# A two-layer float32 transformer kernel: weights of three products woven in pairs and loaded with a step of two, the value product streamed 512 columns wide

## The chip, the cores and the metric

The kernel runs on one core of a Trainium2 chip. The metric is the device time of one execution in microseconds, the median of several runs; lower is better.

## The reference, cut to what matters

Two transformer layers on 256 tokens of width 2048 in float32, at batch 1. The first has stick-breaking and forgetting attention and then PEER: every token picks 16 of 16384 experts in each of 8 heads. The kernel computes the expert part densely: all 16384 expert inputs, weighted by a gate that is zero where an expert isn't picked.

```python
def block(hb):                                   # PEER, first layer
    q = (hb @ w_query).reshape(PEER_BLOCK, PEER_HEADS, 2, D_KEY // 2)
    s = jnp.einsum('thpc,hpnc->thpn', q, sub_keys).astype(jnp.float32)
    top_s, top_i = lax.top_k(s, PEER_TOPK)
    ...
    best_s, best_j = lax.top_k(cand_s, PEER_TOPK)
    idx = jnp.take_along_axis(cand_i, best_j, axis=-1)
    g = jax.nn.softmax(best_s, axis=-1)
    a = jax.nn.gelu(jnp.einsum('thkd,td->thk', jnp.take(u, idx, axis=0), hb), approximate=False)
    return jnp.einsum('thk,thkd->td', (g * a).astype(hb.dtype), jnp.take(v, idx, axis=0))
```

The second layer has block attention, a state-space branch and a feed-forward part of hidden width 5632, with an up projection to 2 x 5632 (`w_up`), a three-tap convolution along the tokens, a gate and a down projection (`w_down`).

## The kernel before, in words

All activations stand transposed, with features on the 128 partitions and the 256 tokens along the free dimension. All large weights come as one stream of 1152 halves (`STREAM`): a half is 128 partitions x 1024 float32, 512 KB. SyncE fetches each half into a ring of four (`raw`). ScalarE copies it, quarter by quarter (512 columns), into a rounded float32r tile `whi` (L1061, L1150), VectorE subtracts to get the low part `wlo` (L1557, L1701; L1901 beside the selection), and TensorE forms each product as three float32r matmuls: high x high, high x low, low x high (`three`, L502, L507, L508; in the value product L651, L659, L661). `whi` and `wlo` hold two halves; semaphore `quarters_used` gives a quarter back to ScalarE, `lo_ready` hands one to TensorE and returns a slot of `raw` to SyncE.

In a dense product (`dense_turn`: expert product `peer_u`, and `w_up`) the weights are the stationary operand, 128 columns of a quarter at a time, and the activations stream, 256 columns. One output chunk of 128 features takes 16 x 3 matmuls. `peer_u` has 128 chunks, `w_up` 88. The first 16 chunks of `w_up` (`early_chunk`) stream 258 columns from the tile `early` while the normalisation is still going on. In the value product (`spread_tokens`, `peer_v`) it is the other way round: the gated expert values of 128 tokens are stationary (`ev_hi`, `ev_lo`) and the weight rows stream, as two sides of 256 columns to a bank; all eight banks of PSUM accumulate over 128 rows of experts. The down product (`spread`, `w_down`) keeps its weights stationary.

Some turns have a cut: one of their matmuls is issued as 240 and 16 columns (`CUT = 240`, the arguments `cuts` and `cut`, the list RESET in the product `w_in_2`).

The activation parts (`parts`, `split_view`) all lie in one area; the third argument is their offset in bytes. The area, `raw`, `whi`, `wlo` and `big` begin at the same residue modulo 256. A row of 256 float32 is 1024 bytes, a row of the first product's tile (`hhi`, 272 columns) 1088. So for the expert product the weights stand 64 bytes after the stream modulo 256 (0 - 192), for the value product also 64 (64 - 0), and for `early`, which begins 80 bytes after a multiple of 256, they stand at 176.

Beside the first half of the expert product, VectorE also selects the experts: `route_turn`, 16 turns, each with 16 low parts (`low`) written out between the steps of the selection. GpSimd then scatters the gates to memory and later multiplies them into the activated values, one expert row per 5.4 us. From turn 14 of the value product on, VectorE adds up the products for the second layer's modulation from 1 MB tiles of `w_mod` (L2030), which GpSimd fetches. After the value product the eight banks go to SBUF, TensorE turns them (L901), and VectorE adds them to `x2` (L2042); this is a stretch in which TensorE waits.

Of the kernel before, what the change touches and what calls it, by code (L numbers as in the profile page):

```python
# [11 lines left out]
ALU = mybir.AluOpType  # L12
# [3 lines left out]
P = 128  # L16
SEQ = 256
# [3 lines left out]
KC = D // P  # L21
HEADS = 8
RING = 4
HALF = 1024
# [5 lines left out]
N_SUB = 128  # L30
# [63 lines left out]
def quarter(q):  # L94

    return slice(q * HALF // 2, (q + 1) * HALF // 2)


def build(nc, d, out):
    ctx = ExitStack()  # L100
    with ctx:
# [9 lines left out]
        at = -(-nc.sbuf_base // 32) * 32  # L111
# [9 lines left out]
        def parts(name, rows, beyond, row=SEQ):  # L121
            return [split_view(name + part, at + k * KC * KEYS * 4 + beyond, rows, row, SEQ)
                    for k, part in enumerate(("_hi", "_lo"))]

        sb_hi, sb_lo = parts("sb_parts", 8, 192)
        tok_hi, tok_lo = parts("tok_parts", KC, 192)
        in_hi_, in_lo_ = parts("in_parts", KC, 192)
        ya_hi, ya_lo = parts("ya_parts", 8, 192)
        at_hi, at_lo = parts("at_parts", 8, 8 * SEQ * 4 + 192)
        mg_hi, mg_lo = parts("mg_parts", 8, 8 * SEQ * 4 + 192)  # L130
        up_hi, up_lo = parts("up_parts", KC, 192)
        dn_hi, dn_lo = parts("dn_parts", 2, 192)
        ev_hi, ev_lo = parts("ev_parts", 2, 64)
        raw = sb("raw", [P, RING, HALF])
        whi = sb("whi", [P, PAIRS, HALF], F32R)
        wlo = sb("wlo", [P, PAIRS, HALF], F32R)
# [33 lines left out]
        PS = ctx.enter_context(nc.psum_tensor("PS", [P, 8, 512], F32))  # L170
# [22 lines left out]
        x2 = region(128 * SEQ - KC * SEQ, KC, SEQ)  # L193
# [303 lines left out]
        def _(pe):  # L497
            CUT = 240
# [47 lines left out]
            def dense_turn(name, chunk0, width, g, after=None, inputs=None, halves=None, shift=0, tiles=None, cuts=()):  # L546

                h0_ = FIRST[name]
                if True:
                    for c in range(4):  # L550
                        pe.wait_ge(banks_free, g * 4 + (chunk0 + c + 1))
                        for half in range(2):
                            for kc in range(8):
                                if kc % 4 == 0:

                                    pe.wait_ge(lo_ready, g * 16 + 2 * (RING + h0_ + 2 * c + half) + kc // 4 + 1)
                                    if inputs is not None and c == 0:
                                        pe.wait_ge(in_ready, inputs + 2 * half + kc // 4 + 1)
                                if tiles is not None and c == 0 and (half + kc == 0 or half * 8 + kc >= 12):
                                    pe.wait_ge(tiles, max(half * 8 + kc + 1, 12))  # L560
                                at_ = slice(kc * P, (kc + 1) * P)
                                hi, lo = tuple(t[:, half * 8:, :] for t in ((tok_hi, tok_lo) if name == "peer_u" else (up_hi, up_lo))) if halves is None else halves[half]
                                last = three(PS[:, (c + shift) % 4, 0:width], whi[:, half, at_], wlo[:, half, at_], hi[:, kc, :], lo[:, kc, :],
                                             half == 0 and kc == 0, half == 1 and kc == 7, c in cuts and half == 0 and kc == 3)
                                if kc % 4 == 3:
                                    last.then_inc(quarters_used, 1)
                        if after is not None:
                            after(c)
# [60 lines left out]
                with pe.Fori(4, turns) as g:  # L629
                    body(g, False, False)  # L630

            def spread_tokens(name, turns, staged, cuts):

                h0_ = FIRST[name]

                def body(g, opening, cut=False):
                    for b in range(4):
                        opens = opening and b == 0
                        e_hi, e_lo = ev_first if opens else (ev_hi[:, b % 2, :], ev_lo[:, b % 2, :])
                        pe.wait_ge(stage_lo, g * 4 + (staged + b + 1))  # L640
                        for half in range(2):
                            if opens:
                                pe.wait_ge(banks_free, 4 + 88 + N_SUB - 2 + 2 * half)
                            for q in range(2):
                                pe.wait_ge(lo_ready, g * 16 + 2 * (RING + h0_ + 2 * b + half) + q + 1)
                                for t in range(2):
                                    o_ = slice(t * P, (t + 1) * P)
                                    for side in range(2):
                                        bank = PS[:, t * 4 + half * 2 + q, side * SEQ:(side + 1) * SEQ]
                                        at_ = slice((2 * q + side) * SEQ, (2 * q + side + 1) * SEQ)  # L650
                                        pe.matmul(bank, e_hi[:, o_], whi[:, half, at_], start=opens and side == 0,  # L651
                                                  stop=False, skip_group_check=True)
                                        if cut and b == 1 and half == 0 and q == 1 and t == 0 and side == 0:
                                            for part in (slice(0, CUT), slice(CUT, SEQ)):
                                                pe.matmul(bank[:, part], e_hi[:, o_],
                                                          wlo[:, half, (2 * q + side) * SEQ + part.start:(2 * q + side) * SEQ + part.stop],
                                                          start=False, stop=False, skip_group_check=True)
                                        else:
                                            pe.matmul(bank, e_hi[:, o_], wlo[:, half, at_], start=False, stop=False,  # L659
                                                      skip_group_check=True)  # L660
                                        last = pe.matmul(bank, e_lo[:, o_], whi[:, half, at_], start=False,  # L661
                                                         stop=False, skip_group_check=True)
                                last.then_inc(quarters_used, 1)

                body(0, True)
                for at, until in zip((0,) + cuts, cuts + (turns,)):
                    if at:
                        body(at, False, True)
                    with pe.Fori(at + 1, until) as g:
                        body(g, False)  # L670

            def mod_sum_rows(acc, count, bank):

# [18 lines left out]
            for g in range(4):  # L692
                pe.wait_ge(squares, g + 1)
                for q in range(4):
                    last = pe.matmul(PS[32 * q:32 * q + 32, 7, 0:KEYS], ones[:, 0:32], sq0[:, 4 * g + q, :], start=g == 0, stop=g == 3)
# [150 lines left out]
            for n in range(KC):  # L846
                pe.wait_ge(banks_free, 56 + n + 1)
                for half in range(2):
                    hi, lo = (fox_hi, fox_lo) if half == 0 else (sb_hi, sb_lo)
                    for kc in range(8):  # L850
# [4 lines left out]
                        at_ = slice(kc * P, (kc + 1) * P)  # L855
# [20 lines left out]
            for n in range(8):  # L876
                t, q4 = n // 4, n % 4
# [14 lines left out]
            mod_turn(2, 7)  # L892
            dense("peer_u", 88, SEQ, (17, 18), cuts=(1,))
            dense("peer_u", 88, SEQ, (18, N_SUB // 4))
            spread_tokens("peer_v", N_SUB // 4, 0, (2, 10, 15, 17, 22, 26))
            for q in range(4):
                pe.wait_ge(acc_copied_a, q + 1)
                pe.wait_ge(acc_copied_v, q + 1)
# [5 lines left out]
            for c in range(KC):  # L904
                q = c % 4
                pe.wait_ge(squares_pv, c // 4 + 1)
                last = pe.matmul(PS[32 * q:32 * q + 32, 0, 0:SEQ], ones[:, 0:32], sqb[:, c, :], start=c < 4, stop=c >= KC - 4)
# [115 lines left out]
            def early_chunk(g, c):  # L1023

                pe.wait_ge(banks_free, 336 + 4 * g + c + (3 if g == 0 and c < 2 else 1))
                for kc in range(KC):
                    half = kc // 8
                    if kc % 4 == 0:
                        pe.wait_ge(lo_ready, 2 * (RING + FIRST["w_up"] + 8 * g + 2 * c + half) + kc // 4 % 2 + 1)
                    if g == 0 and c == 0 and (kc == 0 or kc >= 12):  # L1030
                        pe.wait_ge(early_lo, max(kc + 2, 13))
                    at_ = slice(kc % 8 * P, (kc % 8 + 1) * P)
                    last = three(PS[:, c, 0:SEQ + 2], whi[:, half, at_], wlo[:, half, at_], early[:, 0, kc, 0:SEQ + 2],
                                 early[:, 1, kc, 0:SEQ + 2], kc == 0, kc == KC - 1)
                    if kc % 4 == 3:
                        last.then_inc(quarters_used, 1)
# [502 lines left out]
        def _(dv):  # L1539
# [444 lines left out]
            t = lam_t  # L1984
# [53 lines left out]
            for q in range(4):  # L2038
                dv.wait_ge(acc_turned, q + 1)
                for a in range(2):  # L2040
                    part = x2[:, 4 * q + 2 * a:4 * q + 2 * a + 2, :]
                    i = dv.tensor_tensor(part, part, PS[:, 4 * a + q, :].rearrange("p (b t) -> p b t", b=2), ALU.add)  # L2042
                i.then_inc(x2_ready, 1)
            dv.wait_ge(sums_by_four, 2)
            dv.tensor_scalar(rstd[:, 1, 0:SEQ], PS[:, 0, 0:SEQ], 1.0 / 32, None, ALU.mult).then_inc(sums_kept, 1)
# [420 lines left out]
```

## Time and profile before

| | |
|---|---|
| Median of 3 runs | 3401.7 us (3396.45 to 3410.36) |
| Span of the profiled execution, first to last instruction | 3397.2 us, 4.5 us below that median |
| TensorE busy | 3362.4 us (99%), 29184 matmuls |
| VectorE, ScalarE, GpSimd busy | 2500.3, 1963.3, 736.1 us |
| Mean granted TensorE clock | 0.997 |

"Busy" of TensorE is the time in which at least one matmul was in flight. Matmuls overlap, so their rate is read from how many start in a stretch, or from the times at which they start. A weight load has a row of its own kind (PEld). A releaser is the instruction whose semaphore ended a wait.

### The profile page before, as it was taken

What the parts mean: (1) busy time and instruction counts of PE and PEld (TensorE: products, weight loads), DVE (VectorE), ACT (ScalarE), POOL (GpSimd) and SP (SyncE); (2) the same over time, 40 slices, a digit from 0 to 9 for tenths busy, and PEclk for the clock granted to TensorE, in tenths of its full rate; (3) what the DMA queues carried; (4) which work ended last, traced back from release to release, by engine and by line L of the source; (5) the groups of instructions that cost most, each with busy time, mean ns of one, the idle gap of its engine ahead of it and who ended that gap; (6) DMA issues with size and microseconds to landing.
All of it is one profiled execution on the core that took longest, in us unless ns stands there. A gap on an engine that the chain in (4) does not pass through costs nothing.

```text
span 3397.2 us, 80038 instructions
## 1 busy us (share of the span) xinstructions
PE 3362.4 (99%) x29184; PEld 3319.9 (98%) x29184; DVE 2500.3 (74%) x4438; ACT 1963.3 (58%) x3483; POOL 736.1 (22%) x709
## 2 busy tenths in 40 slices
PE   8999999999999999999999999999999999999999
PEld 7999999999999999999999998999999999999999
DVE  7886688788875555676788879998667776666555
ACT  5456655677765555555555556765565665555554
POOL 1001130377777723555000000000000000000000
PEclk9999999999999999999999999999999999999999
DMA  8867788577777766877898864545555555555555
GB/s 325 335 221 253 248 299 303 161 187 190 186 193 194 194 204 225 271 244 249 320 341 338 335 218 132 176 160 183 162 189 192 187 190 192 192 191 196 187 192 179
DMA packets 234085, 758.61 MB, mean 223 GB/s; under 512 B 60072, under 2 KB 63664, under 8 KB 221104
## 3 DMA queue, kind: packets, MB, share of 16 engines
q1 hardware_dynamic: 167328, 608.57, 52.8%
q0 software_dynamic: 62624, 139.63, 15.0%
q10 hardware_dynamic: 3952, 7.91, 0.7%
q8 instruction: 125, 2.05, 0.2%
q14 instruction: 56, 0.46, 0.0%
HBM read 732.78 MB, written 21.11 MB: 222 GB/s over the span
## 4 chain that ended last, share of the span: by engine, by line
PE 94%; DVE 4%; ACT 1%; issue 1%; DMA 1%; DVEq 0%; SPq 0%; ACTq 0%
PE PS L502 24%; PE PS L508 23%; PE PS L507 23%; PE PS L651 7%; PE PS L661 7%; PE PS L659 7%; DVE wlo L1701 1%; DVE big L1695 0%; PE PS L934 0%; DMA raw<-peer_v_dram 0%; PE PS L761 0%; DVE big L1628 0%; PE PS L923 0%; PE PS L880 0%; PE PS L946 0%
## 5 line engine op out<-in xcount | busy, mean ns | idle before, releaser
L1061 ACT ACTIVATE whi<-raw 128x512 fp32r<-128x512 f32 x1864 | 1157.8, 630 | 1022.8 <-PE PS L508 652.3
L1557 DVE TENSOR_TENSOR wlo<-raw,whi 128x512 fp32r<-128x512 f32 x1480 | 1024.9, 706 | 605.9 <-ACT whi L1061 585.6
L502 PE MATMUL PS<-tok_parts_hi,whi 128*128 128x256 f32 x2048 | 569.4, 278 | 0.8 <-ACT big L1286 0.7
L508 PE MATMUL PS<-tok_parts_hi,wlo 128*128 128x256 f32 x2048 | 568.3, 277 | 0.0
L651 PE MATMUL PS<-whi,ev_parts_hi 128*128 128x256 f32 x2032 | 561.8, 276 | 1.1 <-DVE wlo L1557 1.1
L661 PE MATMUL PS<-whi,ev_parts_lo 128*128 128x256 f32 x2032 | 562.1, 277 | 0.0
L507 PE MATMUL PS<-tok_parts_lo,whi 128*128 128x256 f32 x2030 | 561.7, 277 | 0.0
L659 PE MATMUL PS<-wlo,ev_parts_hi 128*128 128x256 f32 x2026 | 559.9, 276 | 0.0
L1701 DVE TENSOR_TENSOR wlo<-raw,whi 128x512 fp32r<-128x512 f32 x564 | 381.6, 695 | 129.2 <-ACT whi L1150 84.1
L434 POOL DMA_INDIRECT gates_dram<-big x256 | 427.0, 1668 | 200.2 <-issue 91.1
L1150 ACT ACTIVATE whi<-raw 128x512 fp32r<-128x512 f32 x436 | 271.4, 629 | 250.4 <-PE PS L508 247.5
L502 PEld LDWEIGHTS PS<-tok_parts_hi,whi 128*128 128x128 f32 x2048 | 384.6, 188 | 3.8 <-DVE wlo L1901 1.7
L508 PEld LDWEIGHTS PS<-tok_parts_hi,wlo 128*128 128x128 f32 x2048 | 385.4, 188 | 0.0
L651 PEld LDWEIGHTS PS<-whi,ev_parts_hi 128*128 128x128 f32 x2032 | 381.5, 188 | 1.5 <-DVE wlo L1557 1.5
L661 PEld LDWEIGHTS PS<-whi,ev_parts_lo 128*128 128x128 f32 x2032 | 381.5, 188 | 0.0
L507 PEld LDWEIGHTS PS<-tok_parts_lo,whi 128*128 128x128 f32 x2030 | 381.2, 188 | 0.0
L659 PEld LDWEIGHTS PS<-wlo,ev_parts_hi 128*128 128x128 f32 x2026 | 380.9, 188 | 0.0
L508 PE MATMUL PS<-up_parts_hi,wlo 128*128 128x256 f32 x1152 | 318.0, 276 | 0.0
L502 PE MATMUL PS<-up_parts_hi,whi 128*128 128x256 f32 x1152 | 318.0, 276 | 0.0
L507 PE MATMUL PS<-up_parts_lo,whi 128*128 128x256 f32 x1151 | 317.7, 276 | 0.0
L502 PE MATMUL PS<-in_parts_hi,whi 128*128 128x256 f32 x1024 | 289.6, 283 | 5.1 <-DVE wlo L1701 3.2
L508 PE MATMUL PS<-in_parts_hi,wlo 128*128 128x256 f32 x1024 | 286.3, 280 | 0.0
(552 smaller groups left out, 8201.3 us busy)
## 6 DMA issues: line engine op xcount, KB each, us to landing
raw<-peer_u_dram SPq DMA_DIRECT2D x256, 512.0 KB
raw<-peer_v_dram SPq DMA_DIRECT2D x256, 512.0 KB
raw<-w_in_dram SPq DMA_DIRECT2D x240, 512.0 KB
big<-w_mod_dram POOLq DMA_DIRECT2D x96, 1024.0 KB, 6.6
raw<-w_up_dram SPq DMA_DIRECT2D x176, 512.0 KB
raw<-w_down_dram SPq DMA_DIRECT2D x88, 512.0 KB
raw<-w_out_dram SPq DMA_DIRECT2D x64, 512.0 KB
gates_dram<-late POOLq DMA_DIRECT2D x16, 1024.0 KB, 9.0
```

Of the source, the lines that this page charges most:

```text
L434: pool.indirect_dma_start(gates_flat, bass.IndirectOffsetOnAxis(ap=pick_at[:, u, n:n + 1], axis=0), pick_weight[:, u, n:n + 1], None, comp ...
L502: pe.matmul(out, hi, rhi, start=start, stop=False, **more)
L507: pe.matmul(out, hi, rlo, start=False, stop=False, **more)
L508: return pe.matmul(out, lo, rhi, start=False, stop=stop, **more)
L651: pe.matmul(bank, e_hi[:, o_], whi[:, half, at_], start=opens and side == 0, stop=False, skip_group_check=True)
L659: pe.matmul(bank, e_hi[:, o_], wlo[:, half, at_], start=False, stop=False, skip_group_check=True)
L661: last = pe.matmul(bank, e_lo[:, o_], whi[:, half, at_], start=False, stop=False, skip_group_check=True)
L1061: f(whi[:, m % PAIRS, quarter(q)], raw[:, m % RING, quarter(q)], ACT.Copy).then_inc(hi_ready, 1)
L1150: f(whi[:, m % PAIRS, quarter(q)], raw[:, m % RING, quarter(q)], ACT.Copy).then_inc(hi_ready, 1)
L1557: dv.tensor_tensor(wlo[:, m % PAIRS, quarter(q)], raw[:, m % RING, quarter(q)], whi[:, m % PAIRS, quarter(q)], ALU.subtract).then_inc(lo_r ...
L1701: dv.tensor_tensor(wlo[:, m % PAIRS, quarter(q)], raw[:, m % RING, quarter(q)], whi[:, m % PAIRS, quarter(q)], ALU.subtract).then_inc(lo_r ...
```

## The change

1. The weights of `peer_u` and `w_up` are laid out in memory in pairs: within each 256 columns of a half, the columns of two stationary tiles alternate (`woven`). The matmuls read one of the two with a step of two (`dense_turn` without `halves`, and `early_chunk`).
2. The tiles that stream against them begin at offset 96 in place of 192. The weights then stand 160 bytes from the stream modulo 256. `early` isn't moved and stays at 176.
3. In the value product the stationary tile takes every second token, at offset 160 in place of 64. The stream is one matmul of 512 columns in place of two of 256, and the six turns with a cut are gone.
4. As the output rows of the value product are now alternate tokens, the add into `x2` reads and writes `x2` with a step of two.

```diff
-        tok_hi, tok_lo = parts("tok_parts", KC, 192)
+        tok_hi, tok_lo = parts("tok_parts", KC, 96)
-        up_hi, up_lo = parts("up_parts", KC, 192)
+        up_hi, up_lo = parts("up_parts", KC, 96)
-        ev_hi, ev_lo = parts("ev_parts", 2, 64)
+        ev_hi, ev_lo = parts("ev_parts", 2, 160)
...
-                                at_ = slice(kc * P, (kc + 1) * P)
+                                at_ = slice(kc // 2 * 2 * P + kc % 2, (kc // 2 + 1) * 2 * P, 2) if halves is None else slice(kc * P, (kc + 1) * P)
...
                                 for t in range(2):
-                                    o_ = slice(t * P, (t + 1) * P)
-                                    for side in range(2):
-                                        bank = PS[:, t * 4 + half * 2 + q, side * SEQ:(side + 1) * SEQ]
-                                        at_ = slice((2 * q + side) * SEQ, (2 * q + side + 1) * SEQ)
-                                        pe.matmul(bank, e_hi[:, o_], whi[:, half, at_], start=opens and side == 0,
-                                                  stop=False, skip_group_check=True)
...
-                                        last = pe.matmul(bank, e_lo[:, o_], whi[:, half, at_], start=False,
-                                                         stop=False, skip_group_check=True)
+                                    o_ = slice(t, SEQ, 2)
+                                    bank = PS[:, t * 4 + half * 2 + q, :]
+                                    pe.matmul(bank, e_hi[:, o_], whi[:, half, quarter(q)], start=opens, stop=False,
+                                              skip_group_check=True)
+                                    pe.matmul(bank, e_hi[:, o_], wlo[:, half, quarter(q)], start=False, stop=False,
+                                              skip_group_check=True)
+                                    last = pe.matmul(bank, e_lo[:, o_], whi[:, half, quarter(q)], start=False, stop=False,
+                                                     skip_group_check=True)
...
-            spread_tokens("peer_v", N_SUB // 4, 0, (2, 10, 15, 17, 22, 26))
+            spread_tokens("peer_v", N_SUB // 4, 0)
...
-                    at_ = slice(kc % 8 * P, (kc % 8 + 1) * P)
+                    at_ = slice(kc % 8 // 2 * 2 * P + kc % 2, (kc % 8 // 2 + 1) * 2 * P, 2)
...
-                    part = x2[:, 4 * q + 2 * a:4 * q + 2 * a + 2, :]
-                    i = dv.tensor_tensor(part, part, PS[:, 4 * a + q, :].rearrange("p (b t) -> p b t", b=2), ALU.add)
+                    part = x2[:, 4 * q + 2 * a:4 * q + 2 * a + 2, :].rearrange("p b (i t) -> p b t i", t=2)
+                    i = dv.tensor_tensor(part, part, PS[:, 4 * a + q, :].rearrange("p (b t i) -> p b t i", b=2, t=2), ALU.add)
...
+    def woven(w):
+        return w.reshape(-1, P, 4, 2, P).swapaxes(-1, -2).reshape(-1, P, HALF)
```

## Rows read from the trace of the kernel before

**Rows 1.** The page: span, busy time of TensorE, chain of work that ended last.
```profile
span 3397.2 us, 80038 instructions
...
PE 3362.4 (99%) x29184; PEld 3319.9 (98%) x29184; DVE 2500.3 (74%) x4438; ACT 1963.3 (58%) x3483; POOL 736.1 (22%) x709
...
PE 94%; DVE 4%; ACT 1%; issue 1%; DMA 1%; DVEq 0%; SPq 0%; ACTq 0%
```
**Rows 2.** Costliest groups: operation, operands, count | busy us, mean ns | idle before.
```profile
L502 PE MATMUL PS<-tok_parts_hi,whi 128*128 128x256 f32 x2048 | 569.4, 278 | 0.8 <-ACT big L1286 0.7
...
L651 PE MATMUL PS<-whi,ev_parts_hi 128*128 128x256 f32 x2032 | 561.8, 276 | 1.1 <-DVE wlo L1557 1.1
```
**Rows 3.** Windows by stage: stretch, us, busy us and instructions of each engine.
```profile
core 0: us, PE busy (x) PEld busy (x) DVE busy (x) ACT busy (x) POOL busy (x), PEclk, DMA share, GB/s
663.00:977.00 314.00, 313.84 (x2703) 311.26 (x2703) 278.35 (x968) 231.22 (x375) 238.16 (x147) 1.00 0.76 187
977.00:1326.00 349.00, 349.00 (x3079) 349.00 (x3079) 180.91 (x269) 180.57 (x322) 197.42 (x134) 1.00 0.73 200
1331.80:2026.80 695.00, 693.91 (x6103) 693.51 (x6103) 520.67 (x710) 362.66 (x640) 182.11 (x273) 1.00 0.83 291
2664.30:2757.40 93.10, 93.10 (x774) 92.96 (x774) 77.08 (x165) 63.88 (x122) 0.00 (x0) 1.00 0.56 182
2757.40:3149.20 391.80, 391.80 (x3459) 391.80 (x3458) 272.05 (x475) 224.31 (x399) 0.00 (x0) 1.00 0.58 193
3149.20:3391.60 242.40, 242.40 (x2116) 242.28 (x2115) 139.35 (x230) 123.03 (x218) 0.00 (x0) 1.00 0.56 184
```
**Rows 4.** Timeline around a cut, matmul (PE) and weight loads (PEld): start us, us, what.
```profile
2355.00 0.19 PEld L508 LDWEIGHTS PS<-in_parts_hi,wlo 128*128 128x128 f32 x1
2355.11 0.19 PEld L502 LDWEIGHTS PS<-in_parts_hi,whi 128*128 128x128 f32 x1
2355.23 0.19 PEld L504 LDWEIGHTS PS<-in_parts_lo,whi 128*128 128x128 f32 x1
2355.34 0.19 PEld L505 LDWEIGHTS PS<-in_parts_lo,whi 128*128 128x128 f32 x1
2355.45 0.19 PEld L508 LDWEIGHTS PS<-in_parts_hi,wlo 128*128 128x128 f32 x1
2355.56 0.19 PEld L502 LDWEIGHTS PS<-in_parts_hi,whi 128*128 128x128 f32 x1
...
2355.34 0.27 PE L504 MATMUL PS<-in_parts_lo,whi 128*128 128x240 f32 x1
```
**Rows 5.** Timeline of float32 turns (L972, 272 ns each), products (L982, 379 ns; L880).
```profile
2371.74 1.04 PE L972 MATMUL PS<-ident,big 128*128 128x128 f32 x8
...
2385.79 1.89 PE L982 MATMUL PS<-big 128*128 128x256 f32 x8
...
610.02 7.41 PE L880 MATMUL PS<-big 128*128 128x128 f32 x64 [1.78 <-DVE big L1895]
```
**Rows 6.** Timeline of the first product, 272 columns: first and last of nine matmuls.
```profile
124.93 0.29 PE L502 MATMUL PS<-hhi,whi 128*128 128x272 f32 x1
...
125.93 0.29 PE L508 MATMUL PS<-hhi,wlo 128*128 128x272 f32 x1
```
**Rows 7.** VectorE's waits in 660 to 980 us; the selection's line L1924.
```profile
DVE wlo L1901 <- ACT whi L1061: 1.5, 5, 0.4
...
L1924 DVE CAST small_t<-idx x16: 181/205/309, 629.7 to 967.0; 128x32 f32<-128x32 uint32 x16
```
**Rows 8.** 1628 to 1976 us: window, then ScalarE's and TensorE's waits (1326 to 2027).
```profile
1628.00:1976.00 348.00, 347.32 (x3064) 347.12 (x3064) 288.67 (x366) 182.49 (x322) 23.26 (x44) 1.00 0.88 327
...
ACT whi L1061 <- DMA raw<-peer_v_dram: 15.0, 16, 2.3
...
PE PS L651 <- DVE wlo L1557: 1.1, 2, 0.7
```
**Rows 9.** The add after the value product: durations ns min/median/max, first and last start.
```profile
L2042 DVE TENSOR_TENSOR big<-big,PS x8: 677/680/687, 2030.8 to 2035.6; 128x512 f32<-128x512 f32 x8
```

More of the change, by code:

```diff
@@ L630, in spread, with spread_tokens, body @@
                     body(g, False, False)
-            def spread_tokens(name, turns, staged, cuts):
+            def spread_tokens(name, turns, staged):
                 h0_ = FIRST[name]
-                def body(g, opening, cut=False):
+                def body(g, opening):
                     for b in range(4):
@@ L646, in body @@
                                 for t in range(2):
-                                    o_ = slice(t * P, (t + 1) * P)
-                                    for side in range(2):
-                                        bank = PS[:, t * 4 + half * 2 + q, side * SEQ:(side + 1) * SEQ]
-                                        at_ = slice((2 * q + side) * SEQ, (2 * q + side + 1) * SEQ)
-                                        pe.matmul(bank, e_hi[:, o_], whi[:, half, at_], start=opens and side == 0,
-                                                  stop=False, skip_group_check=True)
[L653 to L660, printed above, removed]
-                                        last = pe.matmul(bank, e_lo[:, o_], whi[:, half, at_], start=False,
-                                                         stop=False, skip_group_check=True)
@@ L663, in body @@
+                                    last = pe.matmul(bank, e_lo[:, o_], whi[:, half, quarter(q)], start=False, stop=False,
+                                                     skip_group_check=True)
                                 last.then_inc(quarters_used, 1)
                 body(0, True)
[L666 to L670, printed above, removed]
+                with pe.Fori(1, turns) as g:
+                    body(g, False)
@@ L2423 @@
     a["peer_u"] = np.asarray(peer_u)[0]
-    a["peer_u"] = a["peer_u"].reshape(N_SUB, N_SUB, 2, 8, P).transpose(1, 2, 4, 3, 0).reshape(-1, P, HALF)
+    a["peer_u"] = a["peer_u"].reshape(N_SUB, N_SUB, 2, 8, P).transpose(1, 2, 4, 3, 0)
+    a["peer_u"] = woven(a["peer_u"])
     a["peer_v"] = np.asarray(peer_v)[0].reshape(N_SUB, N_SUB, D).transpose(1, 0, 2)
@@ L2434 @@
     up = chunks(np.asarray(w_up_2)[0]).reshape(2, FC, 2, P, HALF)
-    a["w_up"] = up.transpose(1, 0, 2, 3, 4).reshape(-1, P, HALF)
+    a["w_up"] = woven(up.transpose(1, 0, 2, 3, 4))
     a["w_down"] = rows_of(np.asarray(w_down_2)[0])
```

## The prediction

> **What bounds the kernel now.** [...] The pitch, start to start, is the stretch over its count. Windows cut at the stages [rows 3] give: expert product, second half, 349.0/3079 = 113.3 ns; value product 695.0/6103 = 113.9 ns; up product 391.8/3459 = 113.3 ns; its first 16 chunks (258 columns) 93.1/774 = 120.3 ns, which includes six foreign records; first half of the expert product 314.0/2703 = 116.2 ns. [...]
>
> [...] (b) Where a 256-column matmul is cut into 240 and 16, loads follow each other at 2355.34, .45 and .56, that is 110 ns, where the uncut ones show 113 [rows 4]: the load alone allows about 109.5. [...]
>
> **The change part by part.** *Step of two with distance 160.* [...] Ends for the new pitch of a 256-column matmul: 109.5 (rows 4 and 5, no collision) and 113.3 (nothing changes); between them lie the float32 score products at (7.41 - 0.275)/63 = 113.3, or 111.6 if their one stop of some 0.1 us is taken out; they load and stream at equal pace at distance 0 [rows 5]. [...] I take 109.5, because rows 4 is this very pair of tiles.
>
> [...]
>
> *Expert product.* Its first half doesn't run at TensorE's pace. In 663 to 977 us VectorE waited 1.5 us for ScalarE in all, and the once-a-turn conversion comes 16 times from 629.7 to 967.0, 22.49 us per turn of 192 matmuls, or 117.1 ns each [rows 7]. That is the selection's own instruction stream, untouched by the change. A faster TensorE only arrives at its low parts earlier: 0 us. Ends: 0, and 3072 x (117.1 - 109.5) = -23 if the turn did follow TensorE (VectorE shows 36 us unbusy there); 0 is next to the 1.5 us of waits. Should the pitch rise, this half absorbs it up to 117. Second half: VectorE busy 181 of 349 us, free. 3079 x 109.5 = 337.2 against 349.0: -11.8.
>
> *Value product.* 6144 matmuls of 256 become 3072 of 512. 700.6 us (1326.2 to 2026.8, with the 5.6 us of the opening that stand before the third of rows 3) against 3072 x 215.9 = 663.2, plus the 1.1 us that TensorE waited: -36.3. [...] The six cut turns go: 6 x about 30 ns, nothing. Cover: in 1628 to 1976 us VectorE is busy 288.7 of 348 and the DMA engines 0.88 at 327 GB/s; ScalarE waited 15.0 us for raw halves of peer_v, in 16 waits of up to 2.3 us, while TensorE waited for none of them [rows 8]. At 5% more pace this becomes 0.93 and 344 GB/s. I put +2 us for bursts that reach TensorE; if the queues hold this stretch at its old time, half of the gain is gone (a rival below).
>
> *Up product.* 3459 x 109.5 = 378.8 against 391.8: -13.0 (VectorE 272 of 392, room). First 16 chunks: their moving tile is not moved and stands at 176, but the weights are woven, so the step of two applies; 768 x 110.1 = 84.6 plus six foreign records (0.7) against 93.1: -7.8; ends 0 and -7.8; VectorE would be 77.1/85.3 = 90% busy. I take -6.
>
> *The add behind the value product.* Eight adds on the chain, 680 ns each, now read and write x2 with a step of two [rows 9]. Nearest row: themselves, since a float32 pass of 512 elements takes 0.68 us whatever its order; 0, at worst doubled, +5.4. I take +1.
>
> *What is not touched but shifts.* The down product (2116 in 242.4 us, 114.6 ns) mixes 113.3 and 117.6 ns spells; entering it at another phase may give 239.8 or 248.8: -2.6 to +6.4, taken as 0. The gates' products on GpSimd have 3.7 us of waiting in each 5.4 us. Moved offsets of the parts cost their writers nothing.
>
> Sum: -11.8 - 36.3 + 2 - 13.0 - 6 + 1 = -64.1. The profiled execution's span is 3397.2 and the median 3401.7, 4.5 us around it; 3401.7 - 64.1 = 3337.6, say **3337**.
>
> **Rivals.** *A, half lifted:* the dense pitch goes to 111.6 as in the score products. 3079 and 3459 matmuls gain 1.7 ns each (-5.2, -5.9), the early chunks -4, the value product its -33.3 net of the two additions: 3353. *B, value product alone:* the dense excess isn't a collision but belongs to a 256-column stream beside a 128-column load; only the longer stream gains: 3401.7 - 33.3 = 3368. For it: the up product sits at exactly 113.3 through 3459 matmuls. [...]
> *C, transfers hold the value product:* 1628 to 1976 us keeps its 348 us, the rest gains: -11.8 - 18.3 - 13.0 - 6 + 1 = -48, 3354. For it: DMA share 0.88 with ScalarE waiting; against: TensorE didn't wait.
> *D, slower than before:* the step of two stretches the load, which then is the bound in the dense stages and hides only behind 512 columns. Break-even: 36.3/(3079 + 3459 + 774) = 5.0 ns over 113.3, so from about 118 ns the change loses. [...]
>
> **How the numbers follow.** Forecast 0.45, A 0.17, B 0.15, C 0.09, D 0.09, cancelling near zero 0.05. Half a per cent is 17 us, about what separates a change from none here. Faster: 0.86; same: 0.06; slower: 0.08 (D, less its 3413 end). The range runs from 3316 to 3372: low, the forecast without the +2 and +1, with the early chunks full (-2) and the down product in its good phase (-3) is 3329, and about half of the first half's -23 is left in; high, B and 4 us of the down product's bad phase.
>
> **What would show it.** Right: 977 to the end of the expert product at 109 to 110 ns; 3072 value matmuls 216 ns apart; up product 109 to 110; the selection turns still 22.5 us. Wrong: dense pitch unmoved (B), weight loads more than 110 ns apart in the dense stages (D), TensorE waits for peer_v transfers after mid-value (C), or a selection turn that shortens, which would mean that VectorE wasn't the pace there.

## The result, and the profile after

The changed kernel takes 3474.8 us (median; 3469.9 to 3477.1) against 3400.8 before: a ratio of 1.0215, 95% interval 1.0201 to 1.0229. It is slower by 74 us, where 64 us less were forecast. The same cuts as in [rows 3], stage by stage, in the changed kernel's trace (windows: stretch, us, busy us and instructions of each engine, granted clock, DMA share, GB/s):

```profile
663.00:989.00 326.00, 326.00 (x2719) 326.00 (x2719) 280.13 (x970) 232.56 (x378) 245.71 (x152) 1.00 0.77 182
989.00:1358.70 369.70, 369.70 (x3083) 369.70 (x3082) 181.01 (x268) 181.04 (x323) 179.79 (x129) 1.00 0.71 188
1364.40:2076.30 711.90, 711.40 (x3048) 595.95 (x3047) 523.76 (x710) 362.24 (x640) 181.53 (x273) 1.00 0.82 283
2713.30:2807.90 94.60, 94.60 (x774) 94.50 (x773) 77.17 (x165) 63.83 (x122) 0.00 (x0) 1.00 0.57 179
2807.90:3222.80 414.90, 414.90 (x3460) 414.90 (x3459) 272.73 (x475) 224.37 (x399) 0.00 (x0) 1.00 0.58 182
3222.80:3462.60 239.80, 239.80 (x2115) 239.68 (x2115) 139.25 (x230) 123.02 (x218) 0.00 (x0) 1.00 0.59 186
```

| Stage | before, us | after, us | pitch before, ns | pitch after, ns | forecast, us |
|---|---|---|---|---|---|
| Expert product, first half (beside the selection) | 358.9 | 371.0 | 116.2 | 119.9 | 0 |
| Expert product, second half | 349.0 | 369.7 | 113.3 | 119.9 | -11.8 |
| Value product | 700.6 | 717.5 | 113.9 (256 columns) | 233.6 (512) | -36.3 |
| Up product, first 16 chunks | 93.1 | 94.6 | 120.3 | 122.2 | -6 |
| Up product, rest | 391.8 | 414.9 | 113.3 | 119.9 | -13.0 |
| Down product | 242.4 | 239.8 | 114.6 | 113.4 | 0 |

The six lines make +72; the span grew by 71, from 3397.2 to 3468.2. (The value product counts here from its opening, 1326.2 to 2026.8 before and 1358.8 to 2076.3 after.) No wait explains it. TensorE's waits from the start of the expert product to the turning after the value product, and VectorE's beside the selection (660 to 989 us): engine and line, what it waited for, us in total, times, longest:

```profile
PE PS L890 <- ACT big L1330: 2.1, 1, 2.1
PE PS L502 <- ACT big L1275: 0.7, 1, 0.7
PE PS L649 <- DVE wlo L1546: 0.5, 1, 0.5
...
DVE wlo L1890 <- ACT whi L1050: 13.3, 13, 1.1
```

TensorE is as busy as it was (2156.4 of the 2156.9 us of the six windows), at the same granted clock of 1.00; each matmul simply starts later after the last. VectorE, which waited 1.5 us beside the selection [rows 7], now waits 13.3: it is no longer the pace there.

The first hint at a cause stands at a cut, the counterpart of [rows 4]. Weight loads (PEld) of the changed kernel around 240 + 16 columns: start us, us, what:

```profile
718.75 0.20 PEld L504 LDWEIGHTS PS<-tok_parts_lo,whi 128*128 128x128 f32 x1
718.87 0.20 PEld L505 LDWEIGHTS PS<-tok_parts_lo,whi 128*128 128x128 f32 x1
718.99 0.20 PEld L508 LDWEIGHTS PS<-tok_parts_hi,wlo 128*128 128x128 f32 x1
719.11 0.20 PEld L502 LDWEIGHTS PS<-tok_parts_hi,whi 128*128 128x128 f32 x1
```

Loads that have next to no stream beside them (16 columns, between the last two) still start 0.12 us apart, where it was 0.11 before. The record of a single load has grown too, from 188 to 198 ns on average (expert product, before and then after: count | busy us, mean ns | idle before):

```profile
L502 PEld LDWEIGHTS PS<-tok_parts_hi,whi 128*128 128x128 f32 x2048 | 384.6, 188 | 3.8 <-DVE wlo L1901 1.7
L502 PEld LDWEIGHTS PS<-tok_parts_hi,whi 128*128 128x128 f32 x2048 | 405.9, 198 | 1.1 <-ACT big L1275 0.9
```

With a step of one at the new distance (`plain160` below) it is 190 ns again, so the longer load belongs to the step.

### The profile page after: what moved, and what is told of

It reads as the page before. It is cut to its first block, busy times and chain, and to the rows that moved or that the text cites. A ratio compares the mean times of both kernels' runs of the same rounds, so it can differ in the third digit from the quotient of the medians.

```text
span 3468.2 us, 74016 instructions
## 1 busy us (share of the span) xinstructions
PE 3433.0 (99%) x26106; PEld 3276.7 (94%) x26106; DVE 2505.5 (72%) x4438; ACT 1963.0 (57%) x3483; POOL 724.7 (21%) x709
## 4 chain that ended last, share of the span: by engine, by line
PE 95%; DVE 3%; ACT 1%; DMA 1%; issue 0%; SPq 0%; DVEq 0%; ACTq 0%
PE PS L502 24%; PE PS L508 24%; PE PS L507 23%; PE PS L649 7%; PE PS L651 7%; PE PS L653 7%; DVE wlo L1690 1%; DVE big L1684 0%; PE PS L923 0%; PE PS L750 0%; DVE big L1617 0%; DMA raw<-peer_v_dram 0%; PE PS L912 0%; PE PS L869 0%; PE PS L935 0%
## 5 line engine op out<-in xcount | busy, mean ns | idle before, releaser
L508 PE MATMUL PS<-tok_parts_hi,wlo 128*128 128x256 f32 x2048 | 581.5, 284 | 0.0
L502 PEld LDWEIGHTS PS<-tok_parts_hi,whi 128*128 128x128 f32 x2048 | 405.9, 198 | 1.1 <-ACT big L1275 0.9
L508 PEld LDWEIGHTS PS<-tok_parts_hi,wlo 128*128 128x128 f32 x2048 | 405.8, 198 | 0.0
L649 PE MATMUL PS<-whi,ev_parts_hi 128*128 128x512 f32 x1016 | 402.6, 396 | 0.5 <-DVE wlo L1546 0.5
L651 PE MATMUL PS<-wlo,ev_parts_hi 128*128 128x512 f32 x1016 | 402.3, 396 | 0.0
L507 PEld LDWEIGHTS PS<-tok_parts_lo,whi 128*128 128x128 f32 x2030 | 402.2, 198 | 0.0
L653 PE MATMUL PS<-whi,ev_parts_lo 128*128 128x512 f32 x1016 | 400.3, 394 | 0.0
L507 PE MATMUL PS<-in_parts_lo,whi 128*128 128x256 f32 x1003 | 278.0, 277 | 0.0
L502 PE MATMUL PS<-hhi,whi 128*128 128x272 f32 (+1 forms) x896 | 261.2, 292 | 5.7 <-DVE hlo L1608 4.3
L508 PE MATMUL PS<-hhi,wlo 128*128 128x272 f32 (+1 forms) x896 | 256.5, 286 | 0.0
```

Of the source, the lines that this page charges most:

```text
L502: pe.matmul(out, hi, rhi, start=start, stop=False, **more)
L507: pe.matmul(out, hi, rlo, start=False, stop=False, **more)
L508: return pe.matmul(out, lo, rhi, start=False, stop=stop, **more)
L649: pe.matmul(bank, e_hi[:, o_], whi[:, half, quarter(q)], start=opens, stop=False, skip_group_check=True)
L651: pe.matmul(bank, e_hi[:, o_], wlo[:, half, quarter(q)], start=False, stop=False, skip_group_check=True)
L653: last = pe.matmul(bank, e_lo[:, o_], whi[:, half, quarter(q)], start=False, stop=False, skip_group_check=True)
```

## The experiments

Theories: **L/G**, a load with a step of two is slower in itself and becomes a floor for the dense products; **W**, 160 bytes is merely the wrong distance; **S/Q**, a float32r stream pays in proportion to its own length, so that 512 columns cost well over 216 ns (about 233 under S, 226.7 at best under Q), whatever is loaded. A tick in what follows is 0.4164 ns, measured in `scan2` as what each further column of a bfloat16 stream took: (215.8 - 109.2)/256 ns, or 2.40 columns per ns, at a granted clock of 1.00. No run shows that a float32r column takes one tick; its price is set against that measure. The benches are kernels of their own with only TensorE at work, each run once; a pitch of theirs is a case's stretch over its count of matmuls.

**A bench of distances, `scan1`.** Every case is this loop with other numbers:

```python
for kc in range(8):
    at = slice(kc * P, (kc + 1) * P) if step == 1 else slice(kc // 2 * 2 * P + kc % 2, (kc // 2 + 1) * 2 * P, 2)
    for s_, m_ in ((0, 0), (0, 1), (1, 0)):
        pe.matmul(PS[:, bank, 0:width], st[s_][:, at], mv[m_][:, m0:m0 + width], ...)
```

> A bench, not the transformer: it computes none of the reference. 84 cases of 72 float32r matmuls in the order high-high, high-low, low-high, all with 128x128 stationary tiles, one stretch of time each, nothing else running: stream of 256 or 512 columns, load with a step of one or two, the load 0 to 240 bytes (in steps of 16) after the stream modulo 256; then streams of 16 columns with a step of one, two and four, and a step of four beside 256 and 512 columns, at four distances. [...] Rival W (160 is the wrong distance for a load that keeps pace with the stream): step two beside 256 columns shows a few distances at 109 to 110 ns and others far above 120; 16-column streams cost the same at steps one and two. [...] Rival S (a 512-column stream is slow whatever is loaded beside it): 512 columns with step one about 233, where L and W expect 216 to 220.

Under L, 16-column streams were to go from 110 ns at step one to about 117.5 at step two and further up at step four, and 256 columns at step two never below 117.5.

| Case, 16 distances each | pitch, ns |
|---|---|
| 256 columns, step one | 113.3 at 64 and 144; 116.6 to 120.0 at the other 14 |
| 256 columns, step two | 120.0 at 12; 117.8 at 176, 118.4 at 240, 119.0 at 80, 120.9 at 224; nowhere less |
| 512 columns, step one | 226.7 at 0; 228.9 to 234.7 elsewhere; 233.3 at 64 |
| 512 columns, step two | 226.7 at 16; 230.0 to 233.4 elsewhere; 233.3 at 160 |
| 256 columns, step four | 233.3 at 64, 128 and 192; at 0 the granted clock was still rising (0.81 over the case) |
| 512 columns, step four | 235 to 240 at the four distances tried |

Windows of seven cases of 72 matmuls: 256 columns step one at 64, 256 step two at 160, 512 step one at 0, 512 step one at 64, 512 step two at 160, then step four beside 16 columns at 192 and beside 256 at 128 (columns: stretch, us, TensorE, weight loads, ScalarE, GpSimd, clock, DMA share, GB/s):

```profile
54.46:62.64 8.18, 8.18 (x75) 8.18 (x73) 0.00 (x0) 0.00 (x0) 1.00 0.01 2
...
242.59:251.22 8.63, 8.63 (x74) 8.63 (x73) 0.00 (x0) 0.00 (x0) 1.00 0.00 0
294.22:310.57 16.35, 16.35 (x74) 13.53 (x73) 0.00 (x0) 0.00 (x0) 1.00 0.00 1
361.07:377.87 16.80, 16.80 (x74) 13.49 (x73) 0.00 (x0) 0.00 (x0) 1.00 0.01 1
728.72:745.52 16.80, 16.80 (x74) 14.12 (x72) 0.00 (x0) 0.00 (x0) 1.00 0.00 0
998.52:1015.32 16.80, 16.80 (x73) 16.80 (x74) 0.00 (x0) 0.00 (x0) 0.50 0.00 1
1049.07:1065.87 16.80, 16.80 (x73) 16.80 (x73) 0.00 (x0) 0.00 (x0) 1.00 0.00 0
```

8.18/72 = 113.6 (with its entry), 8.63/72 = 119.9, 16.80/72 = 233.3: the bench repeats the two kernels' pitches without any other engine. W falls, since no distance brings step two to 109 or even to 113. S gains: 512 columns with step one at the old distance cost 233.3. The 16-column cases can't tell step one from step two: the granted clock was 0.51 over 829 to 1015 us (0.50 from 840.6 us on), and both steps cost 213.3 ns there. Only the first 40 matmuls (step one) still had the full clock (0.99 over 829.42 to 833.90 us), and started 112 ns apart. Step four does say something: it costs 233.3 ns at a granted clock of 0.50 and of 1.00 alike (last two lines), so that pace didn't follow TensorE's clock.

**The value product alone, `value512`:** 512 columns, step one, distance 64, cuts of that product gone.

```diff
-                                    for side in range(2):
-                                        bank = PS[:, t * 4 + half * 2 + q, side * SEQ:(side + 1) * SEQ]
...
+                                    bank = PS[:, t * 4 + half * 2 + q, :]
+                                    pe.matmul(bank, e_hi[:, o_], whi[:, half, quarter(q)], start=opens, stop=False,
```

> The kernel before with one part of the change: the value product streams 512 columns, with a step of one and the old distance of 64; the cuts of that product are gone. [...] With a clean long stream 216: -37. Rival S: 233 ns, 717 us, total 3417.

Measured: 3414.3, ratio 1.0037 (1.0023 to 1.0052), slower by 0.4%. Its value product: 3048 matmuls in 711.0 us, 233.3 ns. S was right, and the forecast's 216 and even the 220 at the upper end of L and W were wrong: the longer stream loses without step two and without a new distance.

**Step two at the old distance, `woven64`,** and **step one at the new distance, `plain160`.**

```diff
-        tok_hi, tok_lo = parts("tok_parts", KC, 96)
+        tok_hi, tok_lo = parts("tok_parts", KC, 192)
...
```

> The changed kernel with the three offsets put back to 192, 192 and 64, so step two at the old distance of 64. Theory L: the load alone already sets 117.5 to 120 ns in the dense products and the value product stays at 230 or more: 3460 to 3480. Rival W: the distance decides, so the dense pitch moves clearly away from 120, to anything from 109 to 130: a total that differs from the changed kernel's 3475 by 40 us or more in either direction.

```diff
-                                at_ = slice(kc // 2 * 2 * P + kc % 2, (kc // 2 + 1) * 2 * P, 2) if halves is None else slice(kc * P, (kc + 1) * P)
+                                at_ = slice(kc * P, (kc + 1) * P)
...
```

> The changed kernel with a step of one everywhere and its offsets kept: distance 160, value stream 512 columns, weights not woven. Theory L: dense pitch between the 113.3 at distance 64 and the 119.2 that distance 176 costs in the early chunks; the value product 216 to 226: total 3380 to 3440, below the changed kernel in every case. Rival W, in which step two isn't slow in itself: the same pitch as at distance 160 with step two, 120 and 233, total near 3475.

Measured: woven64 3465.9, ratio 1.0187 (1.0170 to 1.0204); plain160 3471.0, ratio 1.0204 (1.0187 to 1.0221). The up product of each, then the value product of each (windows):

```profile
2808.10:3222.90 414.80, 414.80 (x3459) 414.80 (x3459) 272.50 (x475) 224.38 (x399) 0.00 (x0) 1.00 0.59 182
...
1364.90:2071.60 706.70, 706.39 (x3048) 596.89 (x3048) 520.13 (x710) 362.83 (x640) 186.51 (x273) 1.00 0.84 286
```

```profile
2810.30:3225.00 414.70, 414.70 (x3459) 414.70 (x3458) 272.69 (x475) 224.41 (x399) 0.00 (x0) 1.00 0.59 182
...
1364.60:2075.50 710.90, 710.90 (x3048) 572.26 (x3047) 523.72 (x710) 363.01 (x640) 175.47 (x273) 1.00 0.83 284
```

Either edit of the dense products alone costs all of it: 119.9 ns with step two at 64, and 119.9 with step one at 160. My expectation for plain160 under L (113 to 119, 3380 to 3440 in all) was missed, and its time is the one that W foresaw (near 3475): distance 160 is bad by itself, as the bench says (120.0). W falls again by woven64, whose dense pitch it expected to move clearly away from 120. Both edits put the pitch on the same level, and together they cost no more than one.

**A second bench, `scan2`:** widths, narrow stationary tiles, bfloat16.

```python
CASES = [(w, 128, 1, 64, "") for w in (192, 224, 240, 248, 256, 264, 272, 288, 320, 384, 448, 512)]
CASES += [(w, m, 1, 64, "") for m in (32, 64, 96) for w in (256, 512)]   # and others
```

> The bench again, nothing of the reference computed; 120 matmuls per case, stationary tile of 128 columns, step of one and distance 64 unless said. Cases: streams of 192 to 512 columns; stationary tiles of 32, 64 and 96 columns; the same moving row again and again; bfloat16 tiles at equal byte distances; distances in steps of 4 bytes around 64, 144 and (step two) 176; both tiles shifted together by 16 to 128 bytes; no accumulation, and a new PSUM bank each time; a cut as in the kernel; repeats. Theory Q (a float32r stream pays in proportion to its own length, one tick in 16 columns at best, whatever is loaded): the pitch goes as 17/16 of width/2.4 from 256 to 512 columns, 226.7 at best for 512, and a stationary tile of 32 columns changes little. Theory K (the price is a collision while a load runs, some 7 ns at best): from 256 columns on each further column costs 0.417 ns only, and 32 stationary columns give 109 ns for 256 and 216 for 512. Both expect 113.3 again for 256 columns at distances 64 and 144 and 120 for step two at 160.

| Case (step one, distance 64) | pitch, ns | columns x 0.4164 ns |
|---|---|---|
| 192, 224, 240 columns | 111.7, 111.7, 112.0 | 79.9, 93.3, 99.9 |
| 248, 256, 264, 272 | 116.6, 113.3, 120.0, 123.3 | 103.3, 106.6, 109.9, 113.3 |
| 320, 384, 512 | 146.7, 173.3, 233.3 | 133.2, 159.9, 213.2 |
| 256 and 512 with 32 stationary columns | 113.3, 231.1 | 106.6, 213.2 |
| 256 with 64 and 96 stationary columns | 119.0, 117.2 | 106.6 |
| 256 and 512, no accumulation; a new PSUM bank each time | 113.5, 233.3; 113.4, 233.3 | 106.6, 213.2 |
| 256, both tiles moved by 16, 32 bytes; by 64, 128 bytes | 113.6, 113.6; 117.8, 117.8 | 106.6 |
| 256, distances 56, 60, 68, 72, 136, 140, 148, 152 | 118.6 to 121.8 | 106.6 |
| bfloat16 at distance 64, 256 and 512 | 109.2, 215.8 | 106.6, 213.2 |

Windows of 120 matmuls: 384 columns, 512 columns, 256 columns beside 32 stationary ones, bfloat16 512 (a few of its records are missing, the first among them; the window starts where that one must have):

```profile
156.46:177.26 20.80, 20.80 (x123) 20.80 (x121) 0.00 (x0) 0.00 (x0) 1.00 0.00 1
201.53:229.52 27.99, 27.99 (x121) 22.56 (x120) 0.00 (x0) 0.00 (x0) 1.00 0.00 1
309.28:322.88 13.60, 13.60 (x121) 12.94 (x120) 0.00 (x0) 0.00 (x0) 1.00 0.01 1
...
531.73:557.63 25.90, 25.74 (x119) 11.76 (x120) 0.00 (x0) 0.00 (x0) 1.00 0.00 1
```

K, the collision of the forecast, falls: with a quarter of the load the pitch beside 256 columns is the same (13.60/120 = 113.3, which is 6.7 ns over 256 ticks), tiles of 64 and 96 columns cost more and not less (119.0, 117.2), and what a pitch has over its ticks grows with the stream, to 13.4 ns at 384 columns and 20.1 at 512. Q holds in its main point: from 256 columns on a float32r stream costs 17/16 of its ticks at best (113.3, 226.7), and mostly more (233.3 is 35/32). Its exact form fails, since 384 columns cost 173.3 and not 170. A bfloat16 stream of 512 columns costs 25.90/120 = 215.8. PSUM is ruled out as the cause: without accumulation, or with a new bank each time, the pitches are the same within 0.2 ns (113.5 and 113.4; 233.3). That the price belongs to the stream alone is argued and not shown: every matmul here had a load of its own.

**A distance of 0 for the value product, `value512_d0`,** after the bench, and **two moves within step one, `early64` and `plain144`.**

```diff
-        ev_hi, ev_lo = parts("ev_parts", 2, 64)      # value512
+        ev_hi, ev_lo = parts("ev_parts", 2, 0)       # value512_d0
...
-        early = split_view("early", at_big + 4 * (24 * SEQ + 20), ...)
+        early = split_view("early", at_big + 4 * (24 * SEQ + 48), ...)      # early64
...
-        tok_hi, tok_lo = parts("tok_parts", KC, 192)      # plain144: tok, up; ev to 144
+        tok_hi, tok_lo = parts("tok_parts", KC, 112)
```

> The kernel before with a value product of 512 columns and step one, its stationary tile at distance 0 in place of 64. In the bench that is the only distance at which 512 columns with step one cost 226.7 ns and not 229 to 235. If the bench carries over: 3072 x 226.7 = 696.4 us for the value product against 700.6 before, total 3397 (-4). If the other traffic in the kernel sets it as at distance 64: 233.3 ns, 717 us, total 3414 as in the run with 512 columns at distance 64.

Measured: 3396.8, ratio 0.9993 (0.9983 to 1.0003), value product 3048 in 691.2 us, 226.8 ns: the bench carries over. 512 columns at their best equal two of 256 at theirs.

> The kernel before with one number changed: the streaming tile of the first 16 chunks of the up product begins 112 bytes later, so that the weights stand at 64 after it in place of 176. Distance theory: 258 columns cost 107.5 + 6.7 = 114.2 ns in place of 120, those chunks take 88 us in place of 93, total 3396 to 3399 (-4.5). If the price there comes from the two extra columns and not from the distance: 120 ns still, no change.

Measured: 3401.3, ratio 1.0000 (0.9989 to 1.0010). The early chunks took 93.5 us, not 88: 258 columns gain nothing from the distance that is good for 256 (93.1 us before). Its value product, untouched by the edit, took 703.1 us in this profile (1332.5 to 2035.7) where 695.0 stood before: 2279 of its 6102 matmuls started 116 ns or more apart, where 424 did. So two executions of the same code can differ by 8 us in that product.

> The kernel before with the offsets of the expert, up and value products moved from distance 64 to 144, step one and 256 columns kept. The bench gives 113.3 ns at 64 and 144 alone of 16 distances. If it carries over: same time as before, 3395 to 3405. If only 64 is good in the kernel: dense pitch 117 to 120 and total about 3440 to 3470.

Measured: 3428.5, ratio 1.0082 (1.0067 to 1.0097). Half of it carried over: the expert and up products cost what they did (up: 3458 in 391.7 us, 113.3), while the value product goes to 119.1, although its case in the bench had 113.3:

```profile
1331.20:2058.30 727.10, 727.10 (x6103) 727.10 (x6102) 515.85 (x710) 362.33 (x640) 179.54 (x273) 1.00 0.79 278
2793.70:3185.40 391.70, 391.70 (x3458) 391.70 (x3457) 271.84 (x475) 224.68 (x399) 0.00 (x0) 1.00 0.59 193
```

**A third bench, `scan3b`:** the load alone, and the phase of entry.

```python
CASES = [(w, 128, step, d, "") for step in (1, 2) for w in (160, 192, 224, 240) for d in (64, 160)]
CASES += [(256, 128, 1, 64, "after %d" % k) for k in (16, 32, 48, 64, 96, 128, 160, 192, 208, 224)]   # and others
```

> The bench a third time, nothing of the reference computed. Theory G (with a step of two the load has its own floor): streams of 160 to 240 columns, which are shorter than a load, start about 111.7 ns apart at step one and about 117.5 at step two; with a stationary tile of 32 columns the load is short and step two beside 256 columns comes down to 113.3. Theory O (the woven tiles of odd number begin 4 bytes off the 16-byte grid, and off that grid every distance cost 118.7 or more at step one): step two with even tiles only reaches 113.3 at some of the 16 distances, and narrow streams cost the same at both steps. Theory P (the pitch falls into one of a few levels by the phase in which a stage is entered): step one at distance 64 behind one foreign matmul of 16 to 224 columns shows 113.3 in some cases and 117.8 in others, and step two shows 120 behind all of them.

Windows of 120 matmuls each; in this order 192 columns step one and step two at 64, 240 columns step four, 256 columns step two beside 32 stationary columns at 64, the same at 160, beside 64 stationary columns at 160, 256 columns step two with even tiles only at 160, then step one at 64 entered behind a matmul of 16 and of 32 columns:

```profile
52.70:66.11 13.41, 13.41 (x122) 13.41 (x122) 0.00 (x0) 0.00 (x0) 1.00 0.01 1
161.79:176.01 14.22, 14.22 (x122) 14.22 (x122) 0.00 (x0) 0.00 (x0) 1.00 0.01 1
275.54:303.59 28.05, 28.05 (x122) 28.05 (x121) 0.00 (x0) 0.00 (x0) 0.94 0.00 1
317.72:331.32 13.60, 13.60 (x122) 12.94 (x120) 0.00 (x0) 0.00 (x0) 1.00 0.01 1
331.32:345.39 14.07, 14.07 (x123) 12.97 (x120) 0.00 (x0) 0.00 (x0) 1.00 0.01 1
373.53:387.92 14.39, 14.39 (x122) 14.39 (x121) 0.00 (x0) 0.00 (x0) 1.00 0.00 0
...
589.09:603.49 14.40, 14.40 (x123) 14.40 (x121) 0.00 (x0) 0.00 (x0) 1.00 0.00 1
785.95:800.08 14.13, 14.13 (x122) 14.13 (x121) 0.00 (x0) 0.00 (x0) 1.00 0.00 1
800.08:813.70 13.62, 13.62 (x122) 13.62 (x121) 0.00 (x0) 0.00 (x0) 1.00 0.00 1
```

G holds in its main point. At step one the pitch is 111.7 to 111.8 ns for streams of 160, 192 and 224 columns alike, so what paces these cases is the load: 13.41/120 = 111.8 ns at step one, 14.22/120 = 118.5 at step two (all eight narrow cases lie at 117.5 to 120.0), 28.05/120 = 233.8 at step four. No case with step two and 128 stationary columns came below 117.5 in any bench. With 32 stationary columns instead of 128, step two beside 256 columns comes down to 113.3, though only at distance 64: at 160 and 176 it is 117.2 and 116.7, and 64 stationary columns cost 117.8 at 64 and 120.0 at 160. So the floor of the load (118.5) shuts out 113.3, but the level of 120 at distance 160 stands even with half as many columns to load; the load doesn't explain the last 1 to 2 ns. O falls: even tiles alone cost the same 120.0. P holds: the same tiles at the same addresses run at 117.8 behind 16 columns and at 113.5 behind 32 (five of ten entries gave each level; without a foreign matmul, behind the step-four case, it was 117.8 where the two other benches had 113.3), and step two gave 120.0 behind all five. That puts a limit on the tables of distances above: each entry is one way into the loop, and another way in may give a neighbouring level.

**The dense part alone, `dense_only_b`:** the expert and up products of the changed kernel, the value product as it was.

```diff
-        tok_hi, tok_lo = parts("tok_parts", KC, 192)      # up_parts likewise; ev_parts stay at 64
+        tok_hi, tok_lo = parts("tok_parts", KC, 96)
-                                at_ = slice(kc * P, (kc + 1) * P)
+                                at_ = slice(kc // 2 * 2 * P + kc % 2, (kc // 2 + 1) * 2 * P, 2) if halves is None else slice(kc * P, (kc + 1) * P)
```

> The kernel before with the dense part of the change alone: peer_u and w_up woven, step two, offsets 96; the value product stays at 256 columns, step one, distance 64. If the parts add up by their stages in the two traces (expert product +33, early chunks +2, up product +23, down product -3): about 3455. If the value product's loss depends on the phase in which the dense product leaves it: off by more than 5 us.

Measured: 3461.4, ratio 1.0184 (1.0161 to 1.0206). In its trace the expert product takes 740.8 us and the up product 414.7, the numbers of the changed kernel; the value product 701.1 for 6104 matmuls, with more time at the 117.7 level than before (1937 of them at 116 ns or more, where 424 were). The total is 6 us above my sum, beyond the 5 us that I had allowed, and the value product is where they are; since early64 shows as much with nothing changed there, they say nothing about the edit. Dense part alone +64 us, value product alone +11 (value512), together +74: most of the loss is the dense part.

**The best variant, run more often, `best5`** (the same source as value512_d0).

> The value product with 512 columns, step one and distance 0 again, all else as before, in more rounds: the one variant that came out below the kernel before. Its value product took 696.7 us where 700.6 stood, so -4 us, 3396 against 3400, a ratio of 0.9988. If the two medians so far (3396.8 and 3399.8) were chance, the interval holds 1.

Measured: 3393.2 against 3399.8, ratio 0.9977 (0.9965 to 0.9989). It beats both kernels, by 6.6 us over the one before; its profile shows 3.9 us of that in the value product (700.6 to 696.7) and 2.7 in the down product, which ran in its 113.4 ns level throughout (3145.6 to 3385.2 us). The second part is not a gain of the edit for certain: the same source had 242.3 us there in the profile of `value512_d0`, as the kernel before.

## Why the prediction was wrong, point by point

- **"What bounds the kernel now": right in reading, wrong in cause.** TensorE was the pace (busy 99% of the span, 94% of the chain that ended last [rows 1], granted clock 1.00 in every stage [rows 3]), and the pitches of 113.3 to 120.3 ns were read right. The cause that I had behind the change, a collision of two reads while the load runs, set by their distance, fell in scan2: 256 columns take 113.3 ns beside 32 loaded columns as beside 128, and 119.0 beside 64, and a longer stream pays more (6.7 ns over its ticks at 256 columns, 20.1 at 512). [rows 6] can mislead here. Their 125 ns at 272 columns, (125.93 - 124.93)/8, look like an effect of the distance on top of 113.3; the bench gives 123.3 for 272 columns at the distance of 64 too.
- **"I take 109.5": the step that failed first.** [rows 4] did show the load's floor for the pair of tiles, some 2 ns too low (two gaps at a resolution of 10 ns; scan3b has 111.8) and at step one; the text then carried it to step two, a form of load that no row had. There it is 118.5 ns, 117.5 at the least, above the 113.3 that the dense products already had. I had counted step two as free; it costs 7 ns, and there were 1.5 to give. No run shows the 109.5 at any float32r pitch of 256 columns, nor the 110.1 taken for the 258 columns of the early chunks: the dense products took 119.9 and the chunks 122.2. The new distance was a second mistake of the same size: 160 costs 119.9 with a step of one too. Rival D had the direction and the place (second half +20.7 us, up product +23.1); the long stream, behind which the load was to hide, lost 16.9 us.
- **"3072 x 215.9": the largest single term, wrong by 53 us.** It was taken from float32 matmuls of 256 columns, (1.89 - 0.379)/7 = 215.9 ns [rows 5], for float32r streams of 512. No run shows it for them. Float32 and float32r have different prices: from 128 to 256 columns the float32 pitch grows by (215.9 - 109.7)/128 = 0.83 ns a column [rows 5], while a float32r stream cost 113.3/256 = 0.443 ns a column or more, 17/16 of its ticks, in every case of 256 columns and up; at distance 160 or 64 a stream of 512 costs 233.3 ns, which is worse than 2 x 113.3.
- **The first half of the expert product: the mechanism was right, its bound was passed.** The text said VectorE's turn of 22.49 us absorbs a pitch up to 117. At 119.9 TensorE became the pace: the once-a-turn conversion now comes every 23.2 us (629.9 to 978.0), VectorE waits 13.3 us, +12 us.
- **The break-even of rival D**, "from about 118 ns the change loses", wasn't put to the test: it set the dense loss against 36.3 us won in the value product, which lost instead. With that loss the change loses even at 113.3. The chances were wrong plainly: D had 0.09.
- **Right and small:** the strided adds cost nothing (684 ns each against 680 in [rows 9]); transfers held nothing up (C: TensorE waited 3.3 us in all from 618 to 2080 us, never for a transfer); the down product entered its good level, -2.6 us, which other executions of unchanged code do or don't. Two small slips in the sums, 3337 for 3337.6 and 3316 for the 3317 that the terms of the low end give, change nothing.
- **Rival B** was right that the dense excess isn't a collision, and only half right on what it is: 256 columns cost 113.3 ns beside a load of 32 columns too, so the load of 128 isn't needed for it. Still, the size of the load isn't without effect, as tiles of 64 and 96 columns cost 119.0 and 117.2. B's own number, 3368, failed, as the long stream gained nothing.

What stays open: why a float32r stream pays one tick in sixteen over a column a tick (113.3 ns for 256 columns, 226.7 for 512), what sets the levels 113.3, 117.8 and 120.0, and whether it was the address or the way in that changed the level when both tiles moved together by 64 bytes (117.8) and not by 32 (113.6). The levels are measured; the rule behind them isn't.

## What to carry to other kernels

Where loads and streams alternated one to one here, three floors competed: the load (111.8 ns at step one, 118.5 at step two), the stream (113.3 ns for 256 float32r columns), and the level at which the two settled (113.3, 117.8 or 120.0). A row for one form (step one, float32, 256 columns) is no row for another; before an estimate is carried over to a new access pattern, bench that pattern alone with nothing beside it: a bench of a millisecond shows the 118 and 233 ns at once. A stationary tile of 128 columns read with a step of two took 118.5 ns where a step of one took 111.8 (scan3b); behind a stream of 512 columns the difference could be hidden (226.7 ns at step two and distance 16, as at step one and distance 0, scan1).

## What the runs showed of the hardware

- Loads of 128 float32r columns, one after another: 111.8 ns at step one, 117.5 to 120.0 at step two (scan3b), 233.3 at step four (scan1), at a granted clock of 1.00. At a granted clock of 0.50 steps one and two both take 213.3, and step four still 233.3 (scan1).
- float32r streams of 256 and 512 columns: 113.3 and 226.7 ns at best, 117 to 120 and 229 to 235 at most addresses; bfloat16: 109.2 and 215.8 (scan2).
- The level isn't a function of the distance modulo 256 alone: the same addresses gave 113.5 or 117.8 by the length of one matmul ahead of them, 512 columns with step two at 16 gave 226.7 in two benches and 233.2 in a third, and in the kernel distance 144 was good for two products (113.3) and bad for the third (119.1).
- Over a stretch of streams of 16 columns, each with a load, the granted clock was 0.51 though TensorE counted as busy throughout (185.9 of 185.9 us).
